# A decoder layer on one Trainium2 core: the prompt's value projection by seven block products in place of eight, with VectorE making its operands

## The chip, the cores and the metric

The kernel runs on one core of one Trainium2 chip. The metric is the device time of one execution in microseconds (us), lower is better. Five engines work side by side, each on its own list of instructions, and wait for each other by semaphores: TensorE (PE in the profile; its weight loads PEld), VectorE (DVE), ScalarE (ACT), GpSimd (POOL), and SyncE (SP), which here issues nearly all DMAs.

## The reference

One layer of a hybrid decoder, for a prompt of 512 tokens and for 8 samples of 8 tokens. What the change touches is one slice of the combined input projection, the value `v`:

```
h = rmsnorm(x, norm_pre1) * (1 + sc1[:, None]) + sh1[:, None]
proj = h @ w_in
bg, cg, ua, q, k, v, r, lr, ga, gb = jnp.split(proj, split_idx, axis=-1)
...
v = v.reshape(Bn, T, GLA_HEADS, GLA_DV)
log_a = jax.nn.log_sigmoid((lr @ w_a2 + b_a).astype(jnp.float32)) / GLA_TAU
...
o, gla_state_new = gla_recurrence(q, k, v, log_a, gla_state)
```

`h` is 576 x 1024 (512 prompt tokens, then the 64 tokens of the samples), and the value's part of `w_in` 1024 x 1024. Everything is float32.

## The kernel before

**Products in three parts.** A float32 product is made of three products of rounded numbers: `w_hi` is the weight rounded by a copy on ScalarE (`high`), `w_lo` the rest, a subtraction (`low`, on GpSimd in this part of the kernel); likewise `h_hi` and `h_lo`. TensorE adds hi by hi, lo by hi and hi by lo in PSUM. A weight tile is 128x1024, lies in one of four slots (`w_hi[n % 4]`, `w_lo[n % 4]`), and its raw form lies in `raw[0..1]` or `raw_c[0..5]`. Three semaphores count tiles through that ring: `w_hi_done`, `w_lo_done`, and `ring_free` (TensorE is done with the tile).

**Order of the tiles.** Everything is written out by hand, one program for each engine, in the order in which it is to run. Tiles 0 to 3 are the keys (`TILE_K`), 4 to 7 the queries (`TILE_Q`), then 8 value tiles (`TILE_V`), then 32 tiles of the stage called C1 here (`TILE_C1`: the short convolution's inputs and a gate, eight rounds of four), and so on. Before value tile 0 TensorE needs `w_lo_done` of it, and copies of the keys and queries out of PSUM (`kq_done`).

**The value stage.** For each of 8 value tiles (4 groups of 256 channels, for two halves of 512 columns) `token_tiles` makes for each of four blocks of 128 prompt tokens six matmuls (2 channel blocks by 3 parts) with 512 columns, and for the samples four matmuls from `h_smp_hl`, where hi and lo stand side by side: 28 matmuls a tile, 224 in all. ScalarE copies the results to `v_tok`.

**What ScalarE and VectorE do around it.** The decays need `log_sigmoid(z)`. ScalarE copies |z| to `suf`, and after the copy of the last query tile (tile 7) it does an Exp and a Ln over `suf` (L1050, L1052), each with a load of its function table. The Ln raises `z_abs` to 6. VectorE has `dve.wait_ge(S("z_abs"), 6)`, then `pre - suf` (L1430), then a memset of `suf` (L1432). Behind that it has, in the value stage, only one sum for each half of the samples (L1437). GpSimd makes all `w_lo` of the stage (L893) in a loop.

## Time and profile before

| | us |
|---|---|
| median of 3 runs | 996.61 (996.41 to 996.63) |
| span of the profiled execution | 999.7 |
| TensorE busy in it | 981.8 (98%) |
| VectorE busy | 553.3 (55%) |
| ScalarE busy | 386.1 (39%) |
| GpSimd busy | 221.8 (22%) |

The profiled execution is told by its span alone, from its first to its last instruction; it is 3.1 us longer than the median of the runs without a profile. "L1974" is line 1974 of the kernel before. In a row of the timeline the first number is the start in us, the second how long the row's instructions took together, and what stands in brackets is the idle time of that engine just before, with what ended it. The recorded end of a matmul is modelled: matmuls overlap in the record, so the pace is read from starts, not from durations.

### The profile page before, as it was taken

The numbers are of one execution on the slowest core, as the hardware profiler recorded it, in microseconds if no ns is written. First come the engines' busy times: TensorE is split into PE (matmuls) and PEld (weight loads), VectorE is DVE, ScalarE is ACT, GpSimd is POOL, SyncE is SP. The second block draws the span as 40 slices with busy tenths as digits, with TensorE's granted clock in tenths as the row PEclk, the third lists the DMA queues.
The fourth block names the chain that finished last, engine by engine and source line by source line (L and its number), as shares of the span: only waits on it lengthen the run. The fifth ranks groups of instructions, "written<-read, shape, count | busy, mean of one in ns | idle before, by whom it ended". The sixth has DMA issues, their size and how long they took to land.

```text
span 999.7 us, 18680 instructions
## 1 busy us (share of the span) xinstructions
PE 981.8 (98%) x7719; PEld 894.0 (89%) x7719; DVE 553.3 (55%) x884; ACT 386.1 (39%) x593; POOL 221.8 (22%) x121
## 2 busy tenths in 40 slices
PE   6999999998999999999999999999999999999997
PEld 5889889988999999999998799999999999888886
DVE  2511105575765564436438688777777778760204
ACT  4545333324343333443563345333333334533212
POOL 3043533143343343223343000000000000003430
PEclk9999999999999999999999999999999999999999
DMA  9765344796555757536437043222223222422212
GB/s 325 227 112 172 119 72 112 138 116 125 162 128 155 146 129 134 101 95 162 122 99 213 1 127 86 64 85 85 86 85 85 85 86 64 127 85 85 81 54 94
DMA packets 145028, 115.59 MB, mean 116 GB/s; under 512 B 11225, under 2 KB 121585, under 8 KB 144945
## 3 DMA queue, kind: packets, MB, share of 16 engines
q1 hardware_dynamic: 144849, 114.38, 43.8%
q8 instruction: 61, 1.00, 0.4%
q14 instruction: 22, 0.18, 0.1%
q10 hardware_dynamic: 96, 0.04, 0.0%
HBM read 107.02 MB, written 7.35 MB: 114 GB/s over the span
## 4 chain that ended last, share of the span: by engine, by line
PE 97%; DVE 1%; DMA 1%; ACT 1%; issue 0%; SPq 0%; DVEq 0%; ACTq 0%
PE pair L1974 51%; PE pair L2080 16%; PE pair L2395 10%; PE pair L2348 5%; PE pair L1964 2%; PE pair L2161 1%; PE pair L2134 1%; PE pair L1904 1%; DMA x_tok<-in_x_prompt 1%; PE pair L2072 1%; PE pair L2213 1%; PE pair L2224 1%; PE pair L2073 1%; PE pair L2074 1%; PE pair L2071 1%; PE pair L1916 1%
## 5 line engine op out<-in xcount | busy, mean ns | idle before, releaser
L1974 PE MATMUL pair<-h_hi,w_hi 128*128 128x288 f32 x1264 | 283.1, 301 | 0.1
L1974 PE MATMUL pair<-h_hi,w_lo 128*128 128x288 f32 x1264 | 276.2, 296 | 0.3 <-issue 0.3
L1974 PE MATMUL pair<-h_lo,w_hi 128*128 128x288 f32 x1264 | 276.0, 296 | 0.0
L893 POOL TENSOR_TENSOR w_lo<-raw,w_hi 128x1024 fp32r<-128x1024 f32 x53 | 129.0, 2435 | 556.1 <-ACT w_hi L968 556.1
L1974 PEld LDWEIGHTS pair<-h_hi,w_hi 128*128 128x128 f32 x1264 | 205.2, 189 | 18.4 <-issue 16.7
L1974 PEld LDWEIGHTS pair<-h_hi,w_lo 128*128 128x128 f32 x1264 | 205.6, 189 | 0.5 <-issue 0.5
L1974 PEld LDWEIGHTS pair<-h_lo,w_hi 128*128 128x128 f32 x1264 | 205.8, 189 | 0.0
L968 ACT ACTIVATE w_hi<-raw 128x1024 fp32r<-128x1024 f32 x66 | 69.5, 1057 | 162.2 <-PE pair L2074 81.1
L893 POOL TENSOR_TENSOR w_lo<-raw_c,w_hi 128x1024 fp32r<-128x1024 f32 x24 | 69.7, 2909 | 125.8 <-ACT w_hi L968 125.8
L2080 PE MATMUL pair<-w_hi,f_hi 128*128 128x512 f32 x176 | 68.8, 391 | 0.0
L2080 PE MATMUL pair<-w_lo,f_hi 128*128 128x512 f32 x176 | 68.7, 390 | 0.0
L2080 PE MATMUL pair<-w_hi,f_lo 128*128 128x512 f32 x176 | 68.5, 389 | 0.0
L1217 ACT ACTIVATE cv<-cv 128x592 f32<-128x592 f32 x22 | 15.4, 700 | 106.7 <-DVE cv L536 106.6
L2395 PE MATMUL pair<-t_hi,w_hi 128*128 128x288 f32 x144 | 42.5, 295 | 0.0
L2395 PE MATMUL pair<-t_lo,w_hi 128*128 128x288 f32 x144 | 42.5, 295 | 0.0
L2395 PE MATMUL pair<-t_hi,w_lo 128*128 128x288 f32 x144 | 42.4, 295 | 0.0
L2080 PEld LDWEIGHTS pair<-w_hi,f_hi 128*128 128x128 f32 x176 | 33.1, 188 | 7.1
L2080 PEld LDWEIGHTS pair<-w_hi,f_lo 128*128 128x128 f32 x176 | 33.0, 188 | 7.1
L2080 PEld LDWEIGHTS pair<-w_lo,f_hi 128*128 128x128 f32 x176 | 33.0, 188 | 6.7
L536 DVE SCALAR_TENSOR_TENSOR cv<-ext,ffp,cv 128x592 f32<-128x592 f32 x44 | 36.7, 835 | 1.6
L968 ACT ACTIVATE w_hi<-raw_c 128x1024 fp32r<-128x1024 f32 x24 | 25.2, 1054 | 21.3 <-PE pair L1974 12.9
L2395 PE MATMUL pair<-h_hi,w_hi 128*128 128x288 f32 x108 | 31.8, 294 | 0.0
(351 smaller groups left out, 1618.9 us busy)
## 6 DMA issues: line engine op xcount, KB each, us to landing
raw_c<-in_w_ada SPq DMA_DIRECT2D x32, 512.0 KB, 5.4
raw<-in_w_in SPq DMA_DIRECT2D x224, 64.0 KB, 3.1
raw_c<-in_w_in SPq DMA_DIRECT2D x192, 64.0 KB, 3.6
raw<-in_w_up SPq DMA_DIRECT2D x24, 512.0 KB, 4.8
raw<-in_w_down SPq DMA_DIRECT2D x22, 512.0 KB, 3.8
raw_up<-in_w_up SPq DMA_DIRECT2D x20, 512.0 KB, 3.8
ada_first<-in_w_ada SPq DMA_DIRECT2D x16, 512.0 KB, 9.7
raw<-in_w_in SPq DMA_DIRECT2D x8, 512.0 KB, 5.0
```

Of the source, the lines that this page charges most:

```text
L536: dve.scalar_tensor_tensor(dst[:, :], src[:, tap:tap + CONV], w[tap], dst[:, :], ALU.mult, ALU.add) \
L893: pool.tensor_tensor(lo, raw_tile(n)[:, :], hi.bitcast(F32), ALU.subtract).then_inc(S("w_lo_done"), 1)
L968: act.activation(dst, raw_tile(n)[:, :], ACT.Copy).then_inc(S("w_hi_done"), 1)
L1217: act.activation(cv[:, :], cv[:, :], ACT.Gelu_apprx_tanh).then_inc(S("gelu_done"), 1)
L1904: ins = pe.matmul(one_bank(7 * half)[32 * g:32 * g + 32, 0:256], c_wide[:, i, :], ada_first[:, half, i, 256 * g:256 * g + 256], start=i == ...
L1916: ins = pe.transpose(dst, x_tok[0:n, t, P * m:P * m + P], ident[0:n, 0:n])
L1964: ins = pe.matmul(bank[n][:, half, 0:HALF], w[:, i, :], x[:, i, HALF * half:HALF * half + HALF], start=i == 0 and p == 0, stop=i == KT - 1 ...
L1974: ins = pe.matmul(bank[pair][:, half, 0:HALF], w[:, i, :], x[:, i, HALF * half:HALF * half + HALF], start=i == 0 and p == 0, stop=i == KT ...
L2071: pe.matmul(dst, first_i, wh[:, 0, :], start=first, stop=False)
L2080: ins = pe.matmul(one_bank(banks[t])[0:m, :], x, w[:, i, :], start=first and i == 0 and p == 0, stop=last and i == 1 and p == 2)
L2348: ins = pe.matmul(bank[wo_pair(x)][0:n, c, :], xx, w[:, 512 * c:512 * c + 512], start=y == 0 and p == 0, stop=y == KT - 1 and p == len(pas ...
L2395: ins = pe.matmul(dst, w[:, i, :], x[:, i, :], start=i == 0 and p == 0, stop=i == 3 and p == 2)
```

## The change

The prompt's product `h @ w_v` is cut in halves three ways: tokens (256 and 256), channels (512 and 512), columns (512 and 512). With A11 = first tokens by first channels, A12 = first tokens by second channels, A21 and A22 likewise for the second tokens, and B11, B12, B21, B22 the blocks of the weight (channels by columns), it forms four sums of tokens (A21+A22, that minus A11, A11-A21, and A12 minus the second) and four sums of weights (T1 = B12-B11, T2 = B22-T1, T3 = B22-B12, T4 = B21-T2), and makes seven block products in place of eight. The products go by the weight block that they use, in the order B11, B21, T1, T2, B22, T3, (B12, which serves the samples alone), T4; B11, B21 and T1 open a pair of PSUM banks, the other four go on in a pair that already holds a result. Each block is two tiles `m`, so there are 16 tiles where there were 8: 12 matmuls for the prompt in 14 of them, 4 for the samples in 8 of them, all with 512 columns: 168 + 32 = 200.

The sums of tokens (`token_sums`), their low parts (`s_lo`), the sums of weights (`v_sum`), the low parts of the 16 tiles (`v_low`) and the sums of results (`v_add`) are all on VectorE. ScalarE rounds the 16 tiles and the four sums of tokens. GpSimd makes no low part between tile 7 and the first tile of C1. SyncE loads four blocks of 1 MB instead of eight tiles, and the loads of C1 come after them. The copies out of PSUM and the waits for PSUM follow the new order. The core of the diff:

```
-                    load_ada(n - 2)
+
+            def load_v(kind):
+                half, c0 = {B11: (0, 0), B21: (2, 0), B12: (0, 512), B22: (2, 512)}[kind]
+                for g in range(2):
+                    if kind == B11:
+                        sp.wait_ge(S("w_lo_done"), TILE_V - 1 + g)
+                    sp.dma_start(k2(v_raw(kind, g)), v_w[half + g, :, :, c0:c0 + 512]) \
+                      .then_inc(S(v_in(kind)), 16)
+
+            sp.wait_ge(S("w_lo_done"), 4)
+            for kind in (B21, B11, B12, B22):
+                load_v(kind)
 
             def load_c2(n):
                 load_raw(TILE_C2 + n, in_cols((IN_R, IN_GB)[n % 2] + P * (n // 2)))
 
+            sp.wait_ge(S("v_sum"), v_sums(T4) + 2)
             for n in (TILE_C1, TILE_C1 + 1):
                 load_c1(n)
+            sp.wait_ge(S("w_lo_done"), TILE_V + 2 * T3 + 2)
+            for x in (2, 3):
+                load_ada(x)
+            for n in (TILE_C1 + 2, TILE_C1 + 3):
+                load_c1(n)
+            for x in range(2):
+                sp.wait_ge(S("w_lo_done"), TILE_V + 2 * T4 + x + 1)
+                load_ada(x)
             for i in range(4, 4 * KT):
                 load_c1(TILE_C1 + i)
@@ -901,9 +940,9 @@
             pool.memset(w_a2[:, :], 0.0).then_inc(S("lr_zero"), 1)
             pool.wait_ge(S("w_lo_done"), 3)
             low_of_pair(3)
-            with pool.Fori(1, TILE_C1 // 4) as g:
-                for r in range(4):
-                    low(r, w_hi[r][:, :], w_lo[r][:, :], g * 4 + (r + 1))
+            for r in range(4):
+                low(TILE_Q + r, w_hi[r][:, :], w_lo[r][:, :], TILE_Q + r + 1)
+            pool.wait_ge(S("w_lo_done"), TILE_C1)
             with pool.Fori(TILE_C1 // 4, TILE_C2 // 4) as g:
...
+            def v_high(m):
+                if m >= 16:
+                    high(TILE_V + m)
+                    return
+                kind, g = m // 2, m % 2
+                if kind in (T1, T2, T3, T4):
+                    act.wait_ge(S("v_sum"), v_sums(kind) + g + 1)
+                else:
+                    act.wait_ge(S(v_in(kind)), 48)
+                act.wait_ge(S("ring_free"), TILE_V + m - 3)
+                act.activation(w_hi[m % 4][:, :], v_raw(kind, g)[:, :], ACT.Copy).then_inc(S("w_hi_done"), 1)
+
             for n in range(8):
-                high(n + 3)
+                if n + 3 < TILE_V:
+                    high(n + 3)
+                else:
+                    v_high(n + 3 - TILE_V)
...
+                if n == 3:
+                    act.wait_ge(S("v_sum"), 4)
+                    for i in range(2):
+                        act.activation(s_hi[i][:, :, :], s_32[i][:, :, :], ACT.Copy).then_inc(S("h_hi_done"), 1)
+                if n == 5:
+                    for i in range(2, 4):
+                        act.activation(s_hi[i][:, :, :], s_32[i][:, :, :], ACT.Copy).then_inc(S("h_hi_done"), 1)
...
+            def v_copy(pair, t, c):
+                act.activation(v_tok[:, t:t + 2, 512 * c:512 * c + 512], bank[pair][:, :, :], ACT.Copy).then_inc(S("v_done"), 1)
+
+            for m in range(16):
+                v_high(m + 3)
+                kind = m // 2
+                if m % 2 == 0 or kind in (T3, B22):
+                    continue
+                act.wait_ge(S("ring_free"), TILE_V + m + 1)
+                if kind == B11:
+                    v_copy(V_X, 0, 0)
+                elif kind == T1:
+                    v_copy(V_W, 2, 1)
+                elif kind == T2:
...
+            a11, a12 = (h32[:, 4 * b:4 * b + 4, 0:2 * P] for b in range(2))
+            a21, a22 = (h32[:, 4 * b:4 * b + 4, 2 * P:SEQ] for b in range(2))
+
+            def token_sums():
+                dve.wait_ge(S("h32_act"), 4)
+                dve.wait_ge(S("h_lo_done"), KT)
+                dve.tensor_tensor(s_32[0][:, :, :], a21, a22, ALU.add).then_inc(S("v_sum"), 1)
+                dve.tensor_tensor(s_32[2][:, :, :], a11, a21, ALU.subtract).then_inc(S("v_sum"), 1)
+                dve.wait_ge(S("v_sum"), 1)
+                dve.tensor_tensor(s_32[1][:, :, :], s_32[0][:, :, :], a11, ALU.subtract).then_inc(S("v_sum"), 1)
+                dve.wait_ge(S("v_sum"), 3)
+                dve.tensor_tensor(s_32[3][:, :, :], a12, s_32[1][:, :, :], ALU.subtract).then_inc(S("v_sum"), 1)
+
             for h in range(HEADS):
+                if h == 2:
+                    token_sums()
...
@@ -1424,17 +1506,63 @@
             dve.tensor_copy(mix0[:, :, :].rearrange("p a j -> p (a j)"), one_bank(7)[:, 0:P]).then_inc(S("prm_done"), 1)
             dve.tensor_copy(ff0[:, :, :].rearrange("p a j -> p (a j)"), one_bank(7)[:, P:P + 352]) \
                .then_inc(S("prm_done"), 1)
-            dve.memset(score[:, :, :], 0.0).then_inc(S("zeroed"), 1)
             dve.wait_ge(S("z_abs"), 6)
             dve.wait_ge(S("z_min"), 4)
             dve.tensor_tensor(pre[:, :, :], pre[:, :, :], suf[:, :, :], ALU.subtract).then_inc(S("z_min"), 1)
             dve.wait_ge(S("z_min"), 5)
             dve.memset(suf[:, :, :], 0.0).then_inc(S("level_set"), 1)
             dve.memset(ext[:, 0:2], 0.0).then_inc(S("zeroed"), 1)
-            for c in range(2):
-                dve.wait_ge(S("v_done"), 6 * (c + 1))
+            for i in range(4):
+                dve.wait_ge(S("h_hi_done"), KT + 2 + i + 1)
+                dve.tensor_tensor(s_lo[i][:, :, :], s_32[i][:, :, :], s_hi[i][:, :, :].bitcast(F32), ALU.subtract) \
...
+            def v_low(m):
+                dve.wait_ge(S("w_hi_done"), TILE_V + m + 1)
+                dve.wait_ge(S("w_lo_done"), TILE_V + m)
+                dve.tensor_tensor(w_lo[m % 4][:, :], v_raw(m // 2, m % 2)[:, :], w_hi[m % 4][:, :].bitcast(F32), ALU.subtract) \
...
+            for m in range(16):
+                if m == 7:
+                    v_add(V_V, 0, 0, 1, 2 * B21 + 1)
+                elif m == 9:
+                    v_samples(0)
+                elif m == 13:
+                    v_add(V_W, 0, 1, 5, 2 * B22 + 1)
+                elif m == 15:
+                    v_add(V_X, 2, 1, 4, 2 * T3 + 1)
+                v_low(m)
+                if m == 3:
+                    v_sum(T1, B12, B11)
+                elif m == 5:
+                    v_sum(T2, B22, T1)
+                    v_sum(T4, B21, T2)
+                elif m == 9:
+                    v_sum(T3, B22, B12)
+            dve.memset(score[:, :, :], 0.0).then_inc(S("zeroed"), 1)
+            v_samples(1)
...
+            def v_product(m, pair, block, xs, tokens, first):
...
+                for x in range(2):
+                    at_ = slice(tokens + P * x, tokens + P * x + P)
+                    for i in range(2):
+                        xh, xl = x_hi[:, block + 2 * g + i, at_], x_lo[:, block + 2 * g + i, at_]
+                        for p, (w, xx) in enumerate(((wh, xh), (wl, xh), (wh, xl))):
+                            ins = pe.matmul(bank[pair][:, x, :], xx, w[:, i, :], start=first and g == i == p == 0,
+                                            stop=g == i == 1 and p == 2, skip_group_check=not first)
...
+            plain, sums = (h_hi, h_lo), list(zip(s_hi, s_lo))
+            for m in range(16):
+                kind, g = m // 2, m % 2
+                if g == 0:
+                    if kind == B11:
+                        pe.wait_ge(S("kq_done"), 6)
+                    elif kind == B21:
+                        pe.wait_ge(S("kq_done"), 8)
+                    elif kind == T1:
+                        pe.wait_ge(S("h_lo_done"), KT + 1)
+                    elif kind == T2:
+                        pe.wait_ge(S("h_lo_done"), KT + 2)
+                        pe.wait_ge(S("v_done"), 1)
+                    elif kind == B22:
+                        pe.wait_ge(S("h_lo_done"), KT + 4)
+                        pe.wait_ge(S("v_done"), 4)
+                    elif kind == T3:
+                        pe.wait_ge(S("v_done"), 5)
+                    elif kind == T4:
+                        pe.wait_ge(S("v_summed"), 4)
+                pe.wait_ge(S("w_lo_done"), TILE_V + m + 1)
+                if kind == B11:
+                    v_product(m, V_X, 0, plain, 0, True)
+                    if g == 0:
...
+                    ins = v_smp_product(m, 0, 0, True, False)
+                elif kind == B21:
+                    v_product(m, V_V, 4, plain, 0, True)
...
+                else:
+                    ins = v_product(m, V_X, 4, plain, 2 * P, False)
                 ins.then_inc(S("ring_free"), 1)
```

Three places in the order of instructions matter. The first is VectorE's list from the last operation on z to the first value tile's low part. The names with numbers are buffers; `s_0` and so on are the sums of tokens, `s_lo` their low parts, `raw` and `raw_c` the raw weights. Before:

```order
L1420 TENSOR_SCALAR pre<-pair,prm 128x576 [waits z_abs,z_mm] x4
L1423 COPY ffp<-pair 128x88 [waits rows_tr]
L1424 COPY mix_162<-pair 128x128
L1425 COPY ff_163<-pair 128x352
L1427 MEMSET score 128x2560
L1430 TENSOR_TENSOR pre<-pre,suf 128x2304 [waits z_min,z_abs]
L1432 MEMSET suf 128x2304 [waits z_min]
L1433 MEMSET ext 128x2
L1437 TENSOR_TENSOR v_tok<-v_tok,pair 128x512 [waits v_done] x2
```

The same place after the change, from the copies of parameters on (L1505 to L1507 of the changed kernel are L1423 to L1425 above):

```order
L1507 COPY ff_175<-pair 128x352
L1511 TENSOR_TENSOR pre<-pre,suf 128x2304 [waits z_min,z_abs]
L1513 MEMSET suf 128x2304 [waits z_min]
L1514 MEMSET ext 128x2
L1517 TENSOR_TENSOR s_lo_82<-s_0_86,s_hi_90 128x1024 [waits h_hi_done]
L1517 TENSOR_TENSOR s_lo_83<-s_1_87,s_hi_91 128x1024 [waits h_hi_done]
L1517 TENSOR_TENSOR s_lo_84<-s_2_88,s_hi_92 128x1024 [waits h_hi_done]
L1517 TENSOR_TENSOR s_lo_85<-s_3_89,s_hi_93 128x1024 [waits h_hi_done]
L1523 TENSOR_TENSOR w_lo_55<-raw_49,w_hi_51 128x1024 [waits w_lo_done,w_hi_done]
L1523 TENSOR_TENSOR w_lo_56<-raw_50,w_hi_52 128x1024 [waits w_lo_done,w_hi_done]
```

The memset of `score` has gone further back; four low parts of sums and then the first value tile's low part (L1523) stand behind the instruction that waits for `z_abs`.

The second place is ScalarE's list after the change, from the sixth copy of keys and queries to the fourth value tile (L1089 copies a key or query tile, L1080 rounds a value tile, L1111 and L1113 are the Exp and the Ln, L1103 rounds sums of tokens):

```order
L1080 ACTIVATE w_hi_51<-raw_49 128x1024 [waits ring_free,x_or_v_in0]
L1089 ACTIVATE q<-pair 128x576 [waits ring_free]
L1103 ACTIVATE s_hi_92<-s_2_88 128x1024
L1103 ACTIVATE s_hi_93<-s_3_89 128x1024
L1080 ACTIVATE w_hi_52<-raw_50 128x1024 [waits ring_free,x_or_v_in0]
L1089 ACTIVATE q<-pair 128x576 [waits ring_free]
L1080 ACTIVATE w_hi_53<-raw_c_94 128x1024 [waits ring_free,x_or_v_in1]
L1089 ACTIVATE q<-pair 128x576 [waits ring_free]
L1111 ACT_TABLE_LOAD
L1111 ACTIVATE suf<-suf 128x2304 [waits z_abs]
L1113 ACT_TABLE_LOAD
L1113 ACTIVATE suf<-suf,one 128x2304 [waits z_abs]
```

Exp and Ln stand where they stood, behind the copy of tile 7; only the roundings around them are others.

The third place is GpSimd's list after the change, from the last tile of the pair loads on:

```order
L936 TENSOR_TENSOR w_lo_58<-raw_65,w_hi_54 128x1024 [waits w_hi_done,w_lo_done]
L932 TENSOR_TENSOR w_lo_55<-raw_49,w_hi_51 128x1024 [waits w_hi_done]
L932 TENSOR_TENSOR w_lo_56<-raw_50,w_hi_52 128x1024 [waits w_hi_done]
L932 TENSOR_TENSOR w_lo_57<-raw_49,w_hi_53 128x1024 [waits w_hi_done]
L932 TENSOR_TENSOR w_lo_58<-raw_50,w_hi_54 128x1024 [waits w_hi_done]
L946 UNCONDITIONAL_BRANCH [waits w_lo_done]
```

Behind the four query tiles it now waits until VectorE has made all low parts of the value stage; its loop begins with C1.

## Rows read from the trace of the kernel before

**Rows 1.** The page: span, busy time of three engines.
```profile
span 999.7 us, 18680 instructions
...
PE 981.8 (98%) x7719; PEld 894.0 (89%) x7719; DVE 553.3 (55%) x884; ACT 386.1 (39%) x593; POOL 221.8 (22%) x121
```

**Rows 2.** TensorE's waits in the whole span: us, times, longest.
```profile
PE pair L1870 <- DMA rows_c<-in_c_sample: 6.9, 1, 6.9
PE pair L2134 <- issue: 2.7, 1, 2.7
```

**Rows 3.** Timeline of TensorE: first value matmuls, and first of C1.
```profile
90.78 0.40 PE L2080 MATMUL pair<-w_hi,h_hi 128*128 128x512 f32 x1
...
141.81 0.42 PE L1974 MATMUL pair<-h_hi,w_hi 128*128 128x288 f32 x2
```

**Rows 4.** Timeline of ScalarE, 67 to 100 us.
```profile
71.26 1.06 ACT L968 ACTIVATE w_hi<-raw 128x1024 fp32r<-128x1024 f32 x1 [3.72 <-DMA raw<-in_w_in]
...
78.89 1.06 ACT L968 ACTIVATE w_hi<-raw 128x1024 fp32r<-128x1024 f32 x1 [0.57 <-DMA raw<-in_w_in]
84.58 0.65 ACT L1035 ACTIVATE q<-pair 128x576 f32<-128x576 f32 x1 [4.62 <-PE pair L1974]
...
90.97 0.65 ACT L1035 ACTIVATE q<-pair 128x576 f32<-128x576 f32 x1 [4.16 <-PE pair L1974]
...
92.94 2.13 ACT L1050 ACTIVATE suf<-suf 128x2304 f32<-128x2304 f32 x1
...
96.38 2.22 ACT L1052 ACTIVATE suf<-suf,one 128x2304 f32<-128x2304 f32 x1
```

**Rows 5.** Timeline of VectorE, 54 to 144 us.
```profile
68.08 0.82 DVE L1420 TENSOR_SCALAR pre<-pair,prm 128x576 f32<-128x576 f32 x1 [8.69 <-ACT suf L1040]
...
98.63 2.56 DVE L1430 TENSOR_TENSOR pre<-pre,suf 128x2304 f32<-128x2304 f32 x1 [16.92 <-ACT suf L1052]
101.74 1.98 DVE L1432 MEMSET suf<- 128x2304 f32 x1 [0.55 <-DVE pre L1430]
103.67 0.06 DVE L1433 MEMSET ext<- 128x2 f32 x1
117.73 0.69 DVE L1437 TENSOR_TENSOR v_tok<-v_tok,pair 128x512 f32<-128x512 f32 x1 [14.01 <-ACT v_tok L1067]
```

**Rows 6.** VectorE elsewhere: a group of low parts by form, and two in the timeline.
```profile
L1652 DVE TENSOR_TENSOR w_lo<-raw,w_hi 128x1024 fp32r<-128x1024 f32 x20 | 24.4, 1219 | 0.3
...
606.21 2.55 DVE L1652 TENSOR_TENSOR w_lo<-raw,w_hi 128x1024 fp32r<-128x1024 f32 x2
```

**Rows 7.** Timeline of SP's DMA issues and of GpSimd, value tiles 0 and 1.
```profile
74.83 0.38 SPq L678 DMA_DIRECT2D raw<-in_w_in  x1
75.25 3.79 SPq L681 DMA_DIRECT2D raw_c<-in_w_in  x8
...
80.03 2.40 POOL L893 TENSOR_TENSOR w_lo<-raw,w_hi 128x1024 fp32r<-128x1024 f32 x1 [2.10 <-ACT w_hi L968]
```

**Rows 8.** Timeline of TensorE around its one long wait, and of its first transposes.
```profile
8.37 4.96 PE L1899 MATMUL pair<-ident 128*128 128x128 f32 x22 [1.07 <-DVE c_wide L1324]
...
26.21 1.91 PE L1899 MATMUL pair<-ident 128*128 128x128 f32 x16
...
242.88 0.23 PE L2134 MATMUL pair<-qd,kd 128*32 128x16 f32 x2 [2.72 <-issue]
```

**Rows 9.** Chain that ended last, two of its pieces: start, us.
```profile
232.91 6.59 PE pair L1974 x48
243.11 8.11 PE pair L1974 x48
```

**Rows 10.** Stretches around that wait: busy us of PE, PEld, DVE, ACT, POOL; then granted clock, DMA.
```profile
240.00:241.00 1.00, 0.16 (x18) 0.06 (x6) 0.54 (x1) 0.20 (x1) 0.00 (x0) 1.00 0.90 349
...
244.00:245.00 1.00, 1.00 (x6) 1.00 (x5) 0.00 (x0) 0.00 (x0) 0.94 (x1) 0.50 0.29 98
...
247.00:248.00 1.00, 1.00 (x10) 1.00 (x9) 0.00 (x0) 0.00 (x0) 0.00 (x0) 1.00 0.19 54
```

More of the change, by code:

```diff
@@ L105 @@
 MIXED = (0, 1, 2, 4, 3)
-V_BANK = ((4, 5, 6, 7, 1), (2, 3, 4, 5, 6))
+B11, B21, T1, T2, B22, T3, B12, T4 = range(8)
+V_X, V_V, V_W, V_SMP = 2, 1, 0, 3
 RSTD_O = 2
@@ L167, in layer_program @@
     rows_ada = place("rows_ada", [P, 512], offset=g_at + 88064)
+    s_lo = [place(f"s_lo{i}", [P, 4, 2 * P], F32R, offset=g_at + 36864 + 4096 * i) for i in range(4)]
+    s_32 = [place(f"s_32_{i}", [P, 4, 2 * P], offset=g_at + 36864 + 4096 * i) for i in range(4)]
+    s_hi = [place(f"s_hi{i}", [P, 4, 2 * P], F32R, offset=g_at + at_) for i, at_ in enumerate((53248, 73728, 77824, 81920))]
     raw_c = [place(f"raw_c{i}", [P, 1024], offset=g_at + at_) for i, at_ in
@@ L360, in layer_program, with v_raw, v_sums, v_in @@
         landed_at.append((raw_name(n), so_far[raw_name(n)]))
+    def v_raw(kind, g):
+        first = (raw[0], raw_c[0], raw[0], raw[0], raw_c[4], raw_c[4], raw_c[2], raw_c[0])[kind]
+        second = (raw[1], raw_c[1], raw[1], raw[1], raw_c[5], raw_c[5], raw_c[3], raw_c[1])[kind]
+        return (first, second)[g]
+    def v_sums(kind):
+        return {T1: 4, T2: 6, T4: 8, T3: 10}[kind]
+    def v_in(kind):
+        return f"x_or_v_in{(B11, B21, B12, B22).index(kind)}"
     def raw_landed(n):
@@ L391, in raw_free @@
             return TILE_UP + op_at(FT - 2) + n - TILE_DN + 1
+        if TILE_C1 <= n < TILE_C1 + 2:
+            return TILE_V + 2 * T2 + 2
         if TILE_C1 + 2 <= n < TILE_C1 + 4:
-            return 0
+            return TILE_V + 2 * B12 + 2
         if n in (4, 5):
@@ new lines, in v_low, with v_sum @@
+            def v_low(m):
+                dve.wait_ge(S("w_hi_done"), TILE_V + m + 1)
+                dve.wait_ge(S("w_lo_done"), TILE_V + m)
+                dve.tensor_tensor(w_lo[m % 4][:, :], v_raw(m // 2, m % 2)[:, :], w_hi[m % 4][:, :].bitcast(F32), ALU.subtract) \
+                   .then_inc(S("w_lo_done"), 1)
+            def v_sum(dst, x, y):
+                for g in range(2):
+                    for kind in (x, y):
+                        if kind in (B12, B22):
+                            dve.wait_ge(S(v_in(kind)), 48)
+                        elif kind in (T1, T2):
+                            dve.wait_ge(S("v_sum"), v_sums(kind) + g + 1)
+                    dve.tensor_tensor(v_raw(dst, g)[:, :], v_raw(x, g)[:, :], v_raw(y, g)[:, :], ALU.subtract) \
+                       .then_inc(S("v_sum"), 1)
@@ L2084, in token_tiles @@
                 return ins
-            for n in range(8):
-                c = n // 4
-                pe.wait_ge(S("w_lo_done"), TILE_V + n + 1)
-                if n == 0:
-                    pe.wait_ge(S("kq_done"), 7)
-                    pe.wait_ge(S("z_min"), 4)
-                if n == 4:
-                    pe.wait_ge(S("kq_done"), 8)
-                for tiles in ((0, 1), (2, 3, 4)):
-                    if n == 4 and tiles[0] == 2:
-                        pe.wait_ge(S("v_done"), 3)
-                    if n == 0 and tiles[0] == 2:
+            def v_product(m, pair, block, xs, tokens, first):
+                wh, wl = (k2(w[m % 4]) for w in (w_hi, w_lo))
+                x_hi, x_lo = xs
+                g = m % 2
+                for x in range(2):
[5 more added lines that the diff above has]
+                                            stop=g == i == 1 and p == 2, skip_group_check=not first)
+                return ins
@@ new lines, in v_smp_product @@
+            def v_smp_product(m, c, block, first, last):
+                wh, wl = (k2(w[m % 4]) for w in (w_hi, w_lo))
+                g = m % 2
+                dst = bank[V_SMP][:, c, :]
+                one, two = (h_smp_hl[:, block + 2 * g + i, :] for i in range(2))
+                pe.matmul(dst, one, wh[:, 0, :], start=first and g == 0, stop=False)
+                pe.matmul(dst[0:64, :], one[:, 0:64], wl[:, 0, :], start=False, stop=False)
+                pe.matmul(dst[0:64, :], two[:, 0:64], wl[:, 1, :], start=False, stop=False)
+                return pe.matmul(dst, two, wh[:, 1, :], start=False, stop=last and g == 1)
```

69 lines of the change are left out of this document (41 added, 28 removed).

## The prediction

> **What bounds the kernel now.** I read the page first: TensorE is busy 98% of the span, VectorE 55% [rows 1]. Then TensorE's waits: after its start it has one of any size, 2.7 us, and that one is ended by "issue", so by no engine [rows 2]. Then the chain and the timeline around the value stage. There TensorE does not wait: its first value matmul starts at 90.78 and the first of C1 at 141.81, back to back with its neighbours [rows 3]. That is 51.03 us for 224 matmuls, 0.228 us each. So the stage is bound by the number of matmuls, and every matmul less is worth 0.228 us as long as its operands are there in time. The reader is to see in [rows 4, 5] what those operands will now stand behind. ScalarE copies the last query tile at 90.97, when TensorE has ended it, then does table, Exp, table, Ln until 98.60. VectorE has sat idle for 16.92 us before 98.63 and is released by that Ln. Nobody suffers today, since the low part of value tile 0 was made by GpSimd before that of tile 1, which it did at 80.03 to 82.43 [rows 7], long before 90.78.
>
> **The change part by part.**
>
> *Fewer matmuls.* 224 become 200. 24 x 0.228 = 5.5 us less on TensorE. All have 512 columns like those they replace. Gain 5.5.
>
> *The first low part moves to VectorE's list, behind the wait for z_abs.* This is the term that decides. TensorE's first value matmul waits for `w_lo_done` of tile 0, which is now the first `v_low`. Ahead of it in VectorE's list stand `pre - suf`, the memset of `suf` and four low parts of token sums. `pre - suf` waits for the Ln, the Ln for the copy of tile 7, and that copy for TensorE to end tile 7 at about 90.9: so the whole of it lies after TensorE has run out of work. Nothing there gets quicker: Exp and Ln keep their place on ScalarE. From rows: `pre - suf` starts at 98.63, memsets end at 103.73 [rows 5]. Then four `s_lo` and one `v_low`, each 128x1024. The same form elsewhere takes 1.219, and two of them in a row 2.55 [rows 6], so 1.22 to 1.33 each. I take 1.22, since only the last of the five waits for a count that its own engine raised: 103.73 + 5 x 1.22 = 109.8. TensorE would have started at 90.78. It stalls 19.0 us. With 1.33 it is 19.6. With what VectorE gives back by some 0.04 of overlap between neighbours it is 18.8.
>
> *Can a later instruction pass the one that waits?* The trace before has nothing that shows it: behind `pre - suf` VectorE had only work that came due later. If it could, `v_low` of tile 0 would be done before 90.78 and the sum would be -5.5 alone. I take the order as written, because every row of VectorE's timeline stands in that order. The Trainium skill, "TensorE: Matmul & The Clock Gate", section "Architectural detail: the array is 16× 32×32, not 1× 128×128", says that the queues of ScalarE and VectorE are strictly first in, first out; by that rule the 109.8 stands, and no row here can show it.
>
> *The clock after the stall.* At 240.16 TensorE fell idle for 2.72 us [rows 8]; the granted clock was then 0.50 of full in the stretch from 244 to 245, which is the lower level, 1.2 GHz, and back at 1.00 in 247 to 248 [rows 10]. The 48 matmuls there took 8.11 in place of 6.59 us: 1.5 us [rows 9]. Idleness of 19.0 us is longer, so I expect the same fall. What it costs is what runs before the clock rises. The other bound is the kernel's start, where 22 transposes took 4.96 and later 16 took 1.91: 22 x (0.225 - 0.119) = 2.3 us [rows 8]. If the clock did not fall it would cost 0. I take 1.5, the row that is of the same kind.
>
> *The rest of the value stage.* After the stall VectorE must keep ahead of TensorE: 16 `v_low`, 8 sums of weights, 3 `v_add` of 1.22 (an estimate: a sum of half that size that reads PSUM took 0.69 [rows 5], the 1024-wide form 1.22), two sample sums of 0.69 and the memset of `score`. A tile takes TensorE 12 x 0.228 = 2.7 or 16 x 0.228 = 3.6 us. I wrote the lists of the three engines side by side, ScalarE's rounding at 1.06 [rows 4], TensorE starting at 109.8 with 1.5 for the clock. Tiles 0 to 3 end at 115.0, 118.6, 122.3, 125.9, and TensorE meets their low parts made. The sums T2 and T4 (four operations) delay `v_low` of tile 6 to 128.8; TensorE comes to it at 131.4. T3's sums delay tile 10 to 138.9; TensorE comes at 144.2. The closest place is T4's first tile, which also waits for four sums of results: the third waits for TensorE's tile 9 (144.2), the fourth for its tile 11 (149.6) and ends at 150.9, while TensorE ends tile 13 at 151.4: 0.5 us to spare. Tile 15's low part, 152.2 against 154.2. C1's first tile wants the fifth sum, 155.0, behind the memset, against 156.9. So: no further stall, with the smallest cover 0.5 us. With the long ends of all durations the cover at T4 is still 0.5, since both sides move.
>
> *Early work.* The four token sums (4 x 1.22 to 1.33, about 5.3) go into the 8.69 us in which VectorE is idle before 68.08 [rows 5]: hidden, with 3 us to spare. Two of the roundings of sums go into the 3.72 us before 71.26 on ScalarE, two into the 4.62 before 84.58 [rows 4]. The new loads are one piece of 512 KB where there had been one piece and 8 of 64 KB behind it [rows 7]; B11's second half is issued at 74.83 as tile 1 was, which was rounded at 78.89 [rows 4, 7]. Now tile 0 waits for that half too, 4.5 us later than now, and so does the copy of query tile 5 behind it. Both are wanted at 90.78: hidden by 9 us. Cost 0.
>
> *Loads of C1 behind the stage.* Tiles C1+2 and C1+3 are issued after the low part of tile 13 (146.7), 3.8 us for each eight pieces [rows 7], so issued by 154.3 and landed some 3 us later. TensorE wants C1+2 two tiles of 6.6 us after 156.9, at 170. GpSimd's low part of C1's first tile ends near 154.3 (rounding at 151.7, 2.4 [rows 7]). Cost 0.
>
> *Sum.* First matmul of C1 at 109.8 + 200 x 0.228 + 1.5 = 156.9 in place of 141.81: +15.1 us (19.0 - 5.5 + 1.5). All that follows on TensorE moves with it, for it had no waits from others [rows 2]. On the profiled span, 999.7 + 15.1 = 1014.8. The runs without a profile are 3.1 us below that span, so I add 15.1 to the median: 996.6 + 15.1 = 1011.7.
>
> **The rivals.**
> 1. *As summed*, with its bounds: stall 18.8 to 19.6, clock 1.5 to 2.3, so +14.8 to +16.4; and for what a cover of the early part may hide or a little more waiting, 1009.5 to 1014. Chance 0.74.
> 2. *VectorE falls behind inside the stage.* 31 operations of 128x1024 (4 + 16 + 8 + 3) stand between 103.7 and 155 us, and the cover at T4 is 0.5 us. If each handover between engines costs the 0.55 us that stands before L1432 [rows 5] and not some 0.1, the three or four handovers on the way to T4 and to C1 open a gap of 1 to 2 us, and those on the way sum, rounding, low part at T2 another 1 to 2: 1013 to 1016, and up to 1018 if the clock falls again. Against it: both wait on the same tiles as TensorE and so shift together. Chance 0.12.
> 3. *The clock stays up.* Then 1.5 less: 1010.2. Against it stands [rows 10]. Chance 0.04, inside the range of the first.
> 4. *The 2.7 us of "issue" goes elsewhere.* It stands in the middle of one group of equal matmuls, with DMA share at 0.90 [rows 10], and 24 instructions less may move what causes it. With its slow clock it is 4.2 us: 1007.5 if it vanishes, 1016 if it comes twice. Chance 0.08.
> 5. *Other side: the stall is not there and only the gain is.* The mechanism would be that the first `v_low` is ready when TensorE wants it. Then 996.6 - 5.5 = 991.1. It decides at 96.3: only if that low part is done by 90.8 + 5.5 is the change no loss. But the Ln alone ends at 98.60 [rows 4], and it starts from TensorE's own last tile, so it cannot come earlier unless VectorE runs around its wait. Chance 0.02.
>
> **How the numbers follow.** The likeliest gives 1011.7. The range takes the first, third and most of the second and fourth: 1008.0 to 1016.5. About 0.2% (2 us) is what a measurement of this kernel can tell from no change. Every case but the last is slower by over 0.8%: slower 0.97, same 0.01, faster 0.02.
>
> **What would show it.** In the changed kernel's profile TensorE should have a wait near 19 us ended by VectorE's `w_lo` (L1523) at about 109.8; the granted clock at 0.5 behind it for a few us; VectorE's timeline with `pre - suf` at 98.6 and the four `s_lo` right behind the memsets; then TensorE without a wait over 1 us, 200 matmuls of the value stage and C1 from 156.9 on. The prediction is wrong if `v_low` of tile 0 ends before 98 us; if TensorE's stall is much shorter since Exp and Ln move; or if waits of several us recur at T2, T4 or C1.

## The result and the profile after

The changed kernel takes 1011.45 us (median of 4 runs, 1010.39 to 1012.35), the kernel before 996.51 (4 runs, 995.51 to 996.63). The ratio is 1.0145, with a 95% interval of 1.0125 to 1.0166: slower by 14.9 us, where the forecast was 15.1 us and 1011.7. The profiled execution of the changed kernel took 1012.35 us by its own time, 1.7 us more than its span of 1010.6; the same 1.7 us, to a tenth, lies between time and span in every execution below.

The page first. It answers [rows 1]: the columns are busy time, share of the span and number of instructions of each engine.

```profile
span 1010.6 us, 18686 instructions
...
PE 975.9 (97%) x7695; PEld 888.8 (88%) x7695; DVE 588.2 (58%) x919; ACT 397.3 (39%) x601; POOL 199.2 (20%) x113
```

TensorE is busy less than before by 5.9 us, on 24 matmuls fewer, and its share fell from 98% to 97%. The span grew all the same, so TensorE must stand still somewhere. Its list of waits (total, how many, longest, in us) says where, and answers [rows 2]:

```profile
PE pair L2225 <- DVE w_lo L1523: 18.6, 1, 18.6
PE pair L1998 <- DMA rows_c<-in_c_sample: 7.0, 1, 7.0
PE pair L2044 <- DVE x_tok L1409: 2.0, 1, 2.0
```

One wait of 18.6 us for the low part `w_lo` made at VectorE's L1523 (`v_low`), once, and nothing else that is new but 1.1 us more at L2044, in the kernel's start. (Behind that wait the clock was low for a while too; the experiment with transposes below shows it.) The wait of 2.7 us ended by "issue" isn't in this execution; more on it below.

TensorE's timeline at that place, which answers [rows 3]: first the last matmuls of query tile 7, then the first and last ones of the value stage and the first of C1 (start, duration of the row, in brackets the idle time before it and its releaser).

```profile
91.04 0.42 PE L2102 MATMUL pair<-h_hi,w_lo 128*128 128x288 f32 x2
110.06 0.76 PE L2225 MATMUL pair<-w_hi,h_hi 128*128 128x512 f32 x1 [18.59 <-DVE w_lo L1523]
110.62 0.63 PE L2225 MATMUL pair<-w_lo,h_hi 128*128 128x512 f32 x1
111.04 0.63 PE L2225 MATMUL pair<-w_hi,h_lo 128*128 128x512 f32 x1
...
114.72 0.39 PE L2225 MATMUL pair<-w_hi,h_lo 128*128 128x512 f32 x1
114.94 0.39 PE L2235 MATMUL pair<-w_hi,h_smp_hl 128*128 128x512 f32 x1
...
157.75 0.42 PE L2102 MATMUL pair<-h_hi,w_hi 128*128 128x288 f32 x2
```

Tile 7 ends at about 91.30, the value stage begins at 110.06, C1 at 157.75. In between the starts of the first matmuls are 0.427 us apart and from 114.72 on 0.228. The next rows are windows of the trace: stretch, length, then busy time of PE, PEld, DVE, ACT and POOL with their instructions, and the last three columns are granted clock (PEclk), DMA share and GB/s. They answer [rows 10].

```profile
80.00:90.00 10.00, 10.00 (x77) 10.00 (x77) 0.00 (x0) 5.92 (x7) 0.00 (x0) 1.00 0.51 194
90.00:100.00 10.00, 1.46 (x11) 1.23 (x10) 0.86 (x1) 8.45 (x6) 0.00 (x0) 0.70 0.00 0
100.00:108.00 8.00, 0.00 (x0) 0.00 (x0) 7.45 (x7) 0.05 (x1) 0.00 (x0) 0.50 0.00 0
...
111.00:112.00 1.00, 1.00 (x4) 0.76 (x3) 0.90 (x2) 0.00 (x0) 0.00 (x0) 0.50 0.00 0
...
114.00:115.00 1.00, 1.00 (x5) 0.79 (x4) 1.00 (x2) 0.00 (x0) 0.00 (x0) 0.74 0.00 0
115.00:116.00 1.00, 1.00 (x6) 0.72 (x5) 1.00 (x2) 0.00 (x0) 0.00 (x0) 1.00 0.00 0
```

The granted clock is 1.00 while TensorE works at 80 to 90, has fallen to 0.50 (1.2 GHz of 2.4) within the idle time, stays there when TensorE begins again, and is back at 1.00 from 115 on.

ScalarE at the same place, answering [rows 4]: rounding of value tile 0, copy of query tile 7, Ln.

```profile
80.93 1.06 ACT L1080 ACTIVATE w_hi<-raw 128x1024 fp32r<-128x1024 f32 x1 [5.18 <-DMA raw<-in_w_in]
...
91.50 0.65 ACT L1089 ACTIVATE q<-pair 128x576 f32<-128x576 f32 x1 [4.64 <-PE pair L2102]
...
96.89 2.21 ACT L1113 ACTIVATE suf<-suf,one 128x2304 f32<-128x2304 f32 x1
```

And VectorE, answering [rows 5]:

```profile
99.14 2.56 DVE L1511 TENSOR_TENSOR pre<-pre,suf 128x2304 f32<-128x2304 f32 x1 [19.58 <-ACT suf L1113]
102.25 1.98 DVE L1513 MEMSET suf<- 128x2304 f32 x1 [0.55 <-DVE pre L1511]
104.15 1.22 DVE L1517 TENSOR_TENSOR s_lo<-s,s_hi 128x1024 fp32r<-128x1024 f32 x1
...
105.29 3.49 DVE L1517 TENSOR_TENSOR s_lo<-s,s_hi 128x1024 fp32r<-128x1024 f32 x3
108.69 2.54 DVE L1523 TENSOR_TENSOR w_lo<-raw,w_hi 128x1024 fp32r<-128x1024 f32 x2
...
127.38 1.22 DVE L1523 TENSOR_TENSOR w_lo<-raw,w_hi 128x1024 fp32r<-128x1024 f32 x1
...
150.75 1.22 DVE L1540 TENSOR_TENSOR v_tok<-v_tok,pair 128x1024 f32<-128x1024 f32 x1 [0.41 <-PE pair L2225]
...
155.70 0.63 DVE L1545 TENSOR_TENSOR v_tok<-v_tok,pair 128x512 f32<-128x512 f32 x1
```

The reader should see one chain: TensorE ends tile 7 at 91.30, ScalarE's Ln ends at 99.10, VectorE's `pre - suf` follows it after 19.58 us of idleness, then the memset, four `s_lo`, and the first of the two `v_low` ends at about 109.9, some 0.1 us before TensorE's first value matmul. VectorE was idle when that low part's inputs lay ready (its tile was rounded on ScalarE at 80.93, the last token sum by 84.4): it was not slow, it was waiting.

### The profile page after: what moved, and what is told of

Its sections match the earlier page's. It is cut to its first block, busy times and chain, and to the rows that moved or that the text cites. A ratio compares the mean times of both kernels' runs of the same rounds, so it can differ in the third digit from the quotient of the medians.

```text
span 1010.6 us, 18686 instructions
## 1 busy us (share of the span) xinstructions
PE 975.9 (97%) x7695; PEld 888.8 (88%) x7695; DVE 588.2 (58%) x919; ACT 397.3 (39%) x601; POOL 199.2 (20%) x113
## 4 chain that ended last, share of the span: by engine, by line
PE 95%; DVE 2%; ACT 1%; DMA 1%; issue 0%; SPq 0%; DVEq 0%; ACTq 0%
PE pair L2102 50%; PE pair L2208 12%; PE pair L2579 10%; PE pair L2532 5%; PE pair L2225 4%; PE pair L2092 2%; PE pair L2343 1%; PE pair L2316 1%; DMA x_tok<-in_x_prompt 1%; PE pair L2032 1%; PE pair L2408 1%; PE pair L2397 1%; PE pair L2044 1%; PE pair L2452 1%; PE pair L2412 1%; PE pair L2200 1%
## 5 line engine op out<-in xcount | busy, mean ns | idle before, releaser
L932 POOL TENSOR_TENSOR w_lo<-raw,w_hi 128x1024 fp32r<-128x1024 f32 x45 | 108.6, 2415 | 600.0 <-ACT w_hi L1007 522.7
L1007 ACT ACTIVATE w_hi<-raw 128x1024 fp32r<-128x1024 f32 x58 | 61.1, 1057 | 143.9 <-PE pair L2202 71.0
L932 POOL TENSOR_TENSOR w_lo<-raw_c,w_hi 128x1024 fp32r<-128x1024 f32 x24 | 67.5, 2818 | 114.9 <-ACT w_hi L1007 114.9
L1284 ACT ACTIVATE cv<-cv 128x592 f32<-128x592 f32 x22 | 15.4, 700 | 106.3 <-DVE cv L560 106.2
```

The lines of the kernel that those rows point to most:

```text
L932: pool.tensor_tensor(lo, raw_tile(n)[:, :], hi.bitcast(F32), ALU.subtract).then_inc(S("w_lo_done"), 1)
L1007: act.activation(dst, raw_tile(n)[:, :], ACT.Copy).then_inc(S("w_hi_done"), 1)
L1284: act.activation(cv[:, :], cv[:, :], ACT.Gelu_apprx_tanh).then_inc(S("gelu_done"), 1)
```

## The experiments

**The kernel before, run again.** The profile of before had a 2.7 us "issue" wait inside C1, with a slow clock behind it, that the changed kernel's profile has not. Does it belong to the kernel or to the one execution? No edit.

> The kernel before, unchanged, profiled once more. Theory: the 2.72 us in which TensorE waited for issue at 240 us in the first profile, and the slow clock behind it (1.5 us), belonged to that one execution. Then this profile has no such wait, and its span is 995 to 996 us. Rival: the wait belongs to the program; then it stands again at 240 us and the span is again near 999.7 us.

Measured: 998.92 us, span 997.2. TensorE's waits and the windows around the larger of the two:

```profile
PE pair L2134 <- issue: 1.9, 1, 1.9
...
PE pair L1974 <- issue: 0.8, 1, 0.8
```

```profile
240.00:241.00 1.00, 0.00 (x0) 0.00 (x0) 0.00 (x0) 0.89 (x1) 0.04 (x1) 1.00 0.54 198
241.00:242.00 1.00, 0.74 (x6) 0.72 (x7) 0.47 (x1) 0.00 (x0) 1.00 (x1) 1.00 0.55 188
...
243.00:244.00 1.00, 1.00 (x6) 1.00 (x5) 0.37 (x1) 0.00 (x0) 0.34 (x1) 0.50 0.20 63
```

So the theory "it belongs to that one execution" is wrong as put. Such a wait came again at the same line, this time 1.9 us, with a second one of 0.8, and the clock fell to 0.50 behind it as in [rows 10]; but the DMA share in it was 0.54 where it had been 0.90, so a full DMA isn't what marks it. It varies: 23 further executions of the kernel before have spans of 993.3 to 999.9, with a median of 994.7. Those of 999.7 (the profile shown before the prediction) and 997.2 (this one) are among the long ones, and so are their mean granted clocks among the low ones: 0.997 and 0.998, where 17 of the 23 have 0.999 or more. That speaks against such a wait in most executions, and so in a median, but only the two profiled ones show it directly. None of the six profiled executions of changed kernels (the one above and the five below) has such a wait; the longest for "issue" in any of them is 0.4 us, near 43 us. Whether the change removes it isn't settled by two executions against six, and what causes it stays open.

**One low part ahead of the wait.** Of the change's order in VectorE's list one step is undone: the first `v_low` stands ahead of the wait for `z_abs`.

```
+            v_low(0)
             dve.wait_ge(S("z_abs"), 6)
             ...
-                v_low(m)
+                if m > 0:
+                    v_low(m)
```

> The changed kernel, with the low part of value tile 0 alone moved ahead of the wait for z_abs on VectorE; nothing else. Theory (the order of VectorE's list makes the stall): TensorE starts tile 0 at 91.3 us and ends it at 95.0, then waits for the low part of tile 1, which now stands where that of tile 0 stood, until about 110.0. The stall is 15.0 in place of 18.6 us, the clock falls again, and the kernel is 3.6 us faster than the changed one: about 1007.8 us. Rival (VectorE has too much work, wherever it stands): TensorE reaches C1 no earlier than now, and the time stays at 1011.4 us.

Measured: 1007.29 us (1005.50 to 1008.00, 4 runs) against 996.52 of before on the same chip (13 runs), ratio 1.0098 (1.0079 to 1.0117). TensorE's timeline:

```profile
89.86 0.40 PE L2227 MATMUL pair<-w_hi,h_hi 128*128 128x512 f32 x1
...
108.53 0.79 PE L2227 MATMUL pair<-w_hi,h_hi 128*128 128x512 f32 x1 [14.85 <-DVE w_lo L1512]
```

The first value matmul now follows tile 7 without a gap, at 89.86. One tile later (16 matmuls) TensorE waits 14.85 us, for tile 1's low part, which is still behind the Ln. That is 3.7 us less wait for 3.7 us of work moved into it. What was expected of the wait was 15.0; the time expected, 1007.8, lies within the four runs. The stall is therefore not the price of a tile or of the new arithmetic: it is the place of the wait in VectorE's list.

**Four sums' low parts and three tiles' ahead of the wait.**

```
+            for i in range(4):
+                ... s_lo[i] ...
+            for m in range(3):
+                v_low(m)
             dve.wait_ge(S("z_abs"), 6)
             ...
-                v_low(m)
+                if m > 2:
+                    v_low(m)
```

> The changed kernel, with the four low parts of token sums and the low parts of value tiles 0, 1 and 2 ahead of the wait for z_abs; nothing else. Theory (order): no stall at tile 0. Tile 3 is wanted at 102.2 us and its low part comes behind pre - suf and the memset at about 105.5: a stall of 3.3 us, perhaps with 1.5 us of slow clock; the sums of T2 and T4 then make tile 6 late by about 1.6 us. C1 starts at 142 to 143.5 us in place of 157.75, so 995.5 to 997.5 us. Rival (VectorE's load): the 31 operations of 1.2 us are 37 us of the 45.6 that TensorE needs, so VectorE falls behind at every group of sums, and C1 starts at 148 us or later: 1002 us or more.

Measured: 995.55 us (994.50 to 996.17, 10 runs), ratio 0.9986 (0.9975 to 0.9997): no change that matters against the kernel before, 15.9 us faster than the changed one. VectorE and TensorE:

```profile
98.12 2.56 DVE L1524 TENSOR_TENSOR pre<-pre,suf 128x2304 f32<-128x2304 f32 x1 [8.53 <-ACT suf L1113]
...
103.13 1.22 DVE L1512 TENSOR_TENSOR w_lo<-raw_c,w_hi 128x1024 fp32r<-128x1024 f32 x1
```

```profile
104.40 0.50 PE L2228 MATMUL pair<-w_hi,h_hi 128*128 128x512 f32 x1 [3.00 <-DVE w_lo L1512]
```

Tile 3's low part can't stand ahead of the wait, since ScalarE rounds that tile only after the Ln; so it comes behind the memset, at 103.13, and TensorE waits 3.00 us for it. The clock falls here too, 0.8 us after TensorE has begun again (the starts are 0.43 apart from 105.2 to 108.6), for 8 matmuls: 8 x 0.2 = 1.6 us. The stage takes 50.8 us (90.26 to 141.07) where before it was 51.03: the gain of 5.5 us is there and is given back as 3.0 of stall and about 1.6 of clock; the rest, some 0.6, is a short wait for tile 6 and the overlap that each gap breaks. The 1.6 us expected at T2 came as 0.3: tile 6's low part ends at 115.37, and its first matmul starts at 115.51, 0.52 behind the one before it in place of 0.23. The rival (1002 us or more, C1 at 148 or later) is out.

**TensorE kept busy in the gap.** The order of the changed kernel, and 150 transposes of the identity into a PSUM bank that isn't in use, ahead of the first value matmul:

```
                         pe.wait_ge(S("kq_done"), 6)
+                        keep_warm(150, 4)
```

> The changed kernel, with 150 transposes of the identity into a free PSUM bank on TensorE between its last query tile and value tile 0; their results are overwritten. Theory (the slow clock behind the stall costs 2.1 us): at 0.119 us each they fill 17.9 of the 18.6 us, the granted clock stays at 1.00, value tile 0 still starts at 110.1 us, and the kernel is 2 us faster than the changed one: 1009.4 us. Rival: transposes do not hold the clock up; it falls during them, the rest of them runs at 0.225 us each, value tile 0 starts only at 119 us or later, and the time is 1020 us or more.

Measured: 1010.67 us (1009.01, 1009.69, 1011.65, 1013.72), ratio 1.0147 (1.0123 to 1.0171). The 2 us that were expected (1009.4) don't show in these times: the medians differ by 0.8 us, the four runs lie 4.7 us apart, and the lowest of them is the profiled one. The two longest have a mean granted clock of 0.997 where the profiled one has 1.000; where their clock fell isn't recorded. The trace tells what happens inside the stage, TensorE's timeline and two of the windows:

```profile
90.87 16.54 PE L2027 MATMUL pair<-ident 128*128 128x128 f32 x150
109.54 0.50 PE L2225 MATMUL pair<-w_hi,h_hi 128*128 128x512 f32 x1 [2.14 <-DVE w_lo L1523]
```

```profile
95.00:100.00 5.00, 5.00 (x48) 5.00 (x47) 1.28 (x1) 4.61 (x4) 0.00 (x0) 1.00 0.02 3
...
110.00:115.00 5.00, 5.00 (x24) 3.98 (x23) 4.79 (x5) 0.36 (x1) 0.00 (x0) 1.00 0.01 3
```

The clock stays at 1.00 through the transposes, a remaining wait of 2.14 us and the value stage, which runs from 109.54 to 155.23 in 45.69 us, 200 x 0.228 to 0.1 us. In the changed kernel it takes 47.69. So the clock is worth 2.0 us there. The stall isn't shortened: from tile 7's end at about 90.9 to the first value matmul it is 18.7 us, 16.5 of them filled with transposes, which took 0.110 us each and not 0.119. The Trainium skill, "TensorE: Matmul & The Clock Gate", section "🔬 Part 4: PE-mode transpose", says that transposes don't count as busy in the same way and don't bring the full clock. This trace disagrees, for float32 where the page measured bf16: they held it at 1.00 for 16.5 us. That they also raise a clock that is down is in the profile of the changed kernel, in its start, behind the 2.0 us wait of L2044:

```profile
14.85 3.07 PE L2044 MATMUL pair<-ident,x_tok 128*128 128x128 f32 x16 [2.05 <-DVE x_tok L1409]
```

```profile
16.00:17.00 1.00, 1.00 (x7) 1.00 (x6) 1.00 (x3) 0.75 (x1) 0.00 (x0) 0.50 1.04 381
...
19.00:20.00 1.00, 1.00 (x17) 0.66 (x20) 0.00 (x0) 0.39 (x1) 0.00 (x0) 1.00 1.05 385
```

From 14.85 to 19.50 TensorE ran transposes alone (of the input, and two of the identity). The clock was 0.50 within that time and 1.00 again at 19.0, before any other matmul.

**The low parts back on GpSimd.** The arithmetic of the change stays, but the 16 low parts of weights are GpSimd's, as before, each out of the way of the wait for `z_abs`. One wait had to be added: a sum of weights (`v_sum`) overwrites raw tiles that GpSimd still reads, so VectorE now waits for GpSimd's low part ahead of each group of them.

```
-            pool.wait_ge(S("w_lo_done"), TILE_C1)
+            for m in range(16):
+                pool.wait_ge(S("w_hi_done"), TILE_V + m + 1)
+                pool.tensor_tensor(w_lo[m % 4][:, :], v_raw(m // 2, m % 2)[:, :], ..., ALU.subtract)
...
+                dve.wait_ge(S("w_lo_done"), TILE_V + {T1: 2, T2: 6, T4: 6, T3: 10}[dst])
...
-                v_low(m)
```

> The changed kernel with all 16 low parts of the value tiles on GpSimd again, as before the change (2.4 us each, up to 3.8 where VectorE works beside it); VectorE keeps the sums, the low parts of sums and its place behind z_abs. Theory (the place behind z_abs, not the engine, makes the stall): tiles 0 to 2 start without a wait at 91.3 us. The stall goes to the first thing that still stands behind z_abs, the sums of T1: they end at 110 us, rounding and low part of tile 4 at 113.5, and it is wanted at 105.9, less what tile 3 waited. With one or two more gaps of 1 to 2 us behind the sums of T2, and slow clock after the first, C1 starts at 147 to 151 us: 1001 to 1005 us. Rival (VectorE's load is what matters, and GpSimd takes 20 us off it): no wait above 2 us, C1 at 140 us or earlier, 994 us or less.

Measured: 1002.85 us (1002.12 to 1003.44, 4 runs), ratio 1.0065 (1.0048 to 1.0081) against 996.24 (10 runs) of before on the same chip; time and C1's start are as expected. TensorE's waits, then two of GpSimd's low parts and two pairs of VectorE's sums:

```profile
PE pair L2228 <- POOL w_lo L947: 8.7, 4, 5.7
```

```profile
85.08 2.40 POOL L947 TENSOR_TENSOR w_lo<-raw,w_hi 128x1024 fp32r<-128x1024 f32 x1 [0.97 <-ACT w_hi L1083]
...
99.59 3.79 POOL L947 TENSOR_TENSOR w_lo<-raw_c,w_hi 128x1024 fp32r<-128x1024 f32 x1 [9.75 <-ACT w_hi L1083]
```

```profile
115.24 2.36 DVE L1537 TENSOR_TENSOR raw<-raw_c,raw 128x1024 f32<-128x1024 f32 x2 [4.74 <-POOL w_lo L947]
117.52 4.57 DVE L1537 TENSOR_TENSOR raw_c<-raw_c,raw 128x1024 f32<-128x1024 f32 x2
```

The first value matmul starts at 90.74, unhindered, which shows again what the 18.6 us were. But now there are four waits of 8.7 us in all. Two of them, 1.55 and 5.67 us, come from the place behind the Ln: tile 3 is rounded behind it, and T1's sum VectorE makes only at 108.15, behind the Ln and the `s_lo`; the clock has fallen when that wait ends at 113.03. The other two, 0.25 at tile 7 and 1.23 at tile 14, end with a low part at which GpSimd was still at work; that of tile 14 is the fifth of six that it makes one behind another in 14.19 us. So the place makes most of the loss here, and the slower engine may make a part. C1 starts at 149.03, 58.3 us after the stage's start. GpSimd takes 2.40 us for a low part that has SBUF to itself, and 3.79 for one beside `pre - suf` and the memset; a pair of VectorE's sums takes 2.36 us alone and 4.57 beside a low part on GpSimd. The Trainium skill, "GPSIMD Engine Reference", section "1. Specifications", says that the two share their ways into SBUF and contend where VectorE reads two operands there; these rows agree.

**The wait put where it hurts nobody.** The changed kernel's instructions, all of them, on their own engines; only their order differs. VectorE makes `s_lo`, the low parts of tiles 0 to 2 and T1's sums ahead of the Ln; `pre - suf` and the memset come behind the low part of tile 10; ScalarE rounds tile 3 ahead of the Exp.

```
+            v_high(3)
             act.wait_ge(S("z_abs"), 4)
...
-            dve.wait_ge(S("z_abs"), 6)
-            ...
+            def decays():
+                dve.wait_ge(S("z_abs"), 6)
+                ...
+            sum_low(0)
+            sum_low(1)
+            v_low(0)
+            sum_low(2)
+            sum_low(3)
+            v_low(1)
+            v_sum(T1, B12, B11)
+            v_low(2)
+            for m in range(3, 16):
...
+                if m == 10:
+                    decays()
```

> The changed kernel with VectorE's list in another order, and one rounding on ScalarE moved: low parts of token sums, low parts of value tiles 0, 1 and 2 and the sums of T1 stand in the time before the Ln; tile 3 is rounded before the Exp; the wait for z_abs, pre - suf and the memset of suf come behind the low part of tile 10. The same operations, no more and no less. Theory (order alone): TensorE has no wait above 1 us in the value stage and its clock stays at 1.00, so the stage takes 200 x 0.228 = 45.6 us and the 24 matmuls less come through: C1 starts some 46 to 47 us after value tile 0, 20 us earlier than in the changed kernel, 991 to 992 us, 5 us less than the kernel before. Rival (31 operations on VectorE, 8 for pre - suf and memsets, and 16 + 4 roundings do not fit whatever their order): waits of 1 to 4 us at T2 and T4, and a time of 994 to 997 us, no better than the kernel before.

Measured: 990.26 us (989.57 to 991.32, 5 runs), ratio 0.9943 (0.9929 to 0.9957): 6.0 us faster than the kernel before and 21.2 faster than the changed one, a little better than expected (991 to 992; C1 starts 22.8 us earlier and not 20). VectorE's timeline at the moved place, the first matmuls of the value stage and of C1, and windows of the stage:

```profile
116.67 2.55 DVE L1514 TENSOR_TENSOR pre<-pre,suf 128x2304 f32<-128x2304 f32 x1
119.77 1.98 DVE L1516 MEMSET suf<- 128x2304 f32 x1 [0.55 <-DVE pre L1514]
```

```profile
89.43 0.40 PE L2237 MATMUL pair<-w_hi,h_hi 128*128 128x512 f32 x1
...
135.00 0.42 PE L2114 MATMUL pair<-h_hi,w_hi 128*128 128x288 f32 x2
```

```profile
89.00:99.00 10.00, 10.00 (x47) 8.10 (x46) 1.22 (x1) 9.32 (x7) 0.00 (x0) 1.00 0.01 2
...
109.00:119.00 10.00, 10.00 (x46) 8.17 (x45) 9.90 (x9) 5.03 (x6) 0.00 (x0) 1.00 0.33 93
```

From 89.43 to 135.00 are 45.57 us, 200 matmuls of 0.228, without one wait of TensorE, at a clock of 1.00. VectorE is busy 9.9 of 10 us where it catches up with the moved work, and is still in time. Three things differ from the second experiment on order (tile 3's rounding, T1's sums, the place of `pre - suf`); what each is worth alone was not run. This is the version to keep of those run here.

## Why the prediction was right

**The bound.** Right. TensorE sets the time; each matmul less is worth 0.228 us. 24 x 0.228 = 5.5 was taken, and the stage without waits takes 45.57 where before it took 51.03: 5.46.

**The stall.** Right in mechanism, place and nearly in size: 19.0 was taken, and 110.06 - 91.30 = 18.8 measured. Five operations of 1.22 were taken; in the trace the next starts about 0.1 us before the recorded end of the last (104.15, 105.29, then three in 3.49), so they take 1.14 each: the overlap between neighbours is 0.08 us, twice the 0.04 of the short end of the range. Two `v_low` in a row, the second waiting for the first's count, take 2.54 and not 2.44. Both experiments that move low parts across the wait change the stall as computed from its place (14.85 and 3.00 us).

**Can a later instruction pass the waiting one?** No. VectorE is idle for 19.58 us with `v_low` of tile 0 ready to run. By the rule that the prediction cites from the Trainium skill ("TensorE: Matmul & The Clock Gate", section "Architectural detail: the array is 16× 32×32, not 1× 128×128"), first in, first out, the 109.8 stood, and the trace agrees: 109.9. Moving one `v_low` in the text, and nothing else, moved it in time.

**The clock.** Right in kind, mis-sized: 1.5 was taken from [rows 9], and it cost 2.1: the stage takes 45.57 without waits at a clock of 1.00 (the last experiment), and it took 47.69. Nine intervals of 0.427 in place of 0.228 make 1.8 of it and the first, of 0.56, another 0.3. The bound of 2.3 from the kernel's start was nearer, but not by what was read there: the windows of the kernel before give a granted clock of 1.00 all through those 22 transposes (8.37 to 13.33), so that their 0.225 us each came from a low clock is not shown. Behind the short waits of the kernel before the clock falls only once TensorE is at work again (1.00 in 241 to 242 and 0.50 in 243 to 244, where it resumed at 241.26); behind 18.6 us it is down already when TensorE begins.

**Nothing further inside the stage.** Right: no other wait. Tile 6's low part starts at 127.38 and ends at 128.6 (128.8 was computed). The sum ahead of T4 ends at 151.97 where 150.9 was computed, and TensorE, itself 0.85 later than computed, comes to T4 at 157.75 - 24 x 0.228 = 152.3: the cover was 0.3 us rather than 0.5. The fifth sum ends at 156.3, C1 begins at 157.75. The cover at T4 is thin, but it does not shrink when the rest moves: it is 0.3 us again in the second experiment on order (135.29 against 135.6) and in the last one (129.22 against 129.5), since the sum there waits for TensorE's own tile. That is the reason the prediction gave against rival 2. The 0.55 us that rival 2 set for a handover between engines was misread: L1432 waits there for VectorE's own `pre - suf`. Between engines the trace has 0.04 us (the Ln ends at 99.10, `pre - suf` starts at 99.14) and 0.15 (`v_low` ends at 109.91, the matmul starts at 110.06).

**Early work.** Hidden, as said: the value stage of the changed kernel would have begun 0.5 us later only, and that comes from the input's arrival in the kernel's start (2.0 us for `x_tok` in place of 0.9), which varies from run to run (0.6 in the first experiment on order, 1.8 in the one with GpSimd).

**The sum.** Measured by the two traces within the value stage: 18.76 - 5.47 + 2.13 = 15.4, where 15.1 was forecast: a stall taken 0.2 too long and a clock taken 0.6 too cheap. That the median came within 0.3 us of 1011.7 is better than the terms deserve, since the runs of the changed kernel alone lie 2 us apart. The spans differ by 1010.6 - 999.7 = 10.9 only, mostly because the profiled execution of before holds the 2.7 us wait and its slow clock (4.2 us together) and that of after does not. The prediction added its 15.1 to the median and to the profiled span alike. Only the first was right. It also set a median beside a span, which lie 1.7 us apart: the profiled execution of before was 999.7 + 1.7 = 1001.4, longer than the median by 4.9 and not by 3.1, and most of that is the wait and its clock. Rival 4 took the wait for something that the change could move; the kernel before, run again, shows that its size changes without any change. It stood in both profiled executions of before and in none of the changed kernels, so what rival 4 said of those is neither shown nor refuted.

## What to carry to other kernels

Before work is moved to an idle engine, read what that engine is waiting for, not how busy it is: VectorE was 55% busy and idle for 17 us before the place, and that idleness was the danger, because the new work stood behind the wait which made it. If the engine that starves is also the one which the wait's releaser depends on (TensorE ends tile 7, then Exp and Ln, then VectorE), the whole length of that chain can go on the end of the program, as the 18.6 us did here. The same instructions in another order gave 21 us back here, so a new arithmetic should be judged only after the waits in the list that feeds it have been placed behind the operands that the bounding engine needs first.
